# A block of attention and expert lookup on one core: TensorE's signal for a finished pair of expert sums moves from the pair's last product to a drain behind it

## What is computed

```python
def expert_chunk(args):
    xc, ic, gc = args
    u = jnp.take(u_tab, ic, axis=0)
    a = jnp.einsum('chkd,cd->chk', u, xc)
    wgt = gc * jax.nn.gelu(a)
    vv = jnp.take(v_tab, ic, axis=0)
    return jnp.einsum('chk,chkd->cd', wgt, vv)
```

## Time and profile before

| | |
|---|---|
| median of three runs | 1384.9 us |
| span of the profiled execution | 1366.9 us |
| what lies around the span (difference) | 18.0 us |
| TensorE busy | 1199.9 us, 88% |
| VectorE busy | 861.8 us, 63% |
| GpSimd busy | 500.2 us, 37% |
| ScalarE busy | 420.2 us, 31% |
| mean granted TensorE clock | 0.969 |
| moved by DMA | 405.66 MB |

### The profile page before, as it was taken

The page is one execution under the profiler, slowest core; times in us unless marked ns, Lnnn a source line. Parts: engine busy times, 40 slices in busy tenths (PEclk is TensorE's granted clock), DMA queues, the critical chain, the costliest instruction groups (busy, mean ns, idle before and its releaser), DMA issues. The chain is left out here.

```text
span 1366.9 us, 14592 instructions
## 1 busy us (share of the span) xinstructions
PE 1199.9 (88%) x4663; PEld 665.4 (49%) x4663; DVE 861.8 (63%) x1765; ACT 420.2 (31%) x1138; POOL 500.2 (37%) x580
## 2 busy tenths in 40 slices
PE   7899888888778978876788889789999999999997
PEld 4676554433344542222345433236544545999443
DVE  2657669574663654776746557679989543676345
ACT  2213334344223343343423324432323311222000
POOL 1000356666665666766666666630000000000000
PEclk9999999999998999999999999999999999999999
DMA  9998789999998999999999999986644444454450
GB/s 358 390 349 326 286 319 339 367 357 367 364 366 300 406 403 405 407 377 364 340 371 353 400 405 409 377 306 233 224 139 148 145 150 156 157 175 145 175 184 31
DMA packets 134303, 405.66 MB, mean 297 GB/s; under 512 B 10153, under 2 KB 11585, under 8 KB 133971
## 3 DMA queue, kind: packets, MB, share of 16 engines
q0 software_dynamic: 75024, 273.19, 53.1%
q1 hardware_dynamic: 57860, 127.48, 25.8%
q10 hardware_dynamic: 1342, 4.06, 0.8%
HBM read 403.12 MB, written 1.05 MB: 296 GB/s over the span
## 5 line engine op out<-in xcount | busy, mean ns | idle before, releaser
L1143 PE MATMUL psum<-gathered,modr 128*128 128x512 f32 x1024 | 505.0, 633 | 130.3 <-DMA gathered<-in_peer_v_dram,expert_idx 49.0
L2489 DVE CUSTOM_DVE_ANT_0 gathered<-gathered,psum 128x1024 f32<-128x1024 f32 x256 | 311.5, 1217 | 202.3 <-DMA gathered<-in_peer_u_dram,expert_idx 153.3
L1143 PEld LDWEIGHTS psum<-gathered,modr 128*128 128x128 f32 x1024 | 190.7, 199 | 404.7 <-issue 284.9
L687 POOL DMA_INDIRECT gathered<-in_peer_u_dram,expert_idx x256 | 244.9, 957 | 240.5 <-DVE expert_idx L1997 144.0
L701 POOL DMA_INDIRECT gathered<-in_peer_v_dram,expert_idx x256 | 242.6, 947 | 169.9 <-remote 73.7
L780 PE MATMUL psum<-featT,weight_ring 128*128 128x128 f32 (+2 forms) x960 | 145.3, 305 | 14.4 <-issue 11.3
L780 PEld LDWEIGHTS psum<-featT,weight_ring 128*128 128x128 f32 x960 | 133.7, 196 | 43.9 <-issue 35.6
L780 PE MATMUL psum<-weight_ring,featT 128*128 128x512 f32 x336 | 147.9, 596 | 1.3 <-ACT featT L1563 0.8
L1737 ACT ACTIVATE gel<-dots 128x1 f32<-128x1 f32 x256 | 51.1, 200 | 255.1 <-issue 128.1
L1746 ACT ACTIVATE modr<-ident,wgt 128x128 f32<-128x128 f32 x256 | 102.8, 402 | 18.5 <-issue 1.1
L780 PEld LDWEIGHTS psum<-weight_ring,featT 128*128 128x128 f32 x336 | 62.6, 190 | 78.8 <-issue 76.6
(11 more groups left out here) (443 smaller groups left out, 1343.1 us busy)
## 6 DMA issues: line engine op xcount, KB each, us to landing
weight_ring<-in_w_in_dram SPq DMA_DIRECT2D x16, 2048.0 KB
weight_ring<-in_w_up_dram SPq DMA_DIRECT2D x8, 2048.0 KB
weight_ring<-in_w_down_dram SPq DMA_DIRECT2D x8, 2048.0 KB
weight_ring<-in_ada_w_dram SPq DMA_DIRECT2D x5, 2048.0 KB
work<-in_ada_w_dram SPq DMA_DIRECT2D x5, 2048.0 KB, 16.3
weight_ring<-in_peer_wq_dram SPq DMA_DIRECT2D x3, 2048.0 KB
gathered<-in_ada_w_dram SPq DMA_DIRECT2D x2, 2048.0 KB, 14.5
gathered<-in_peer_u_dram,expert_idx POOLq DMA_INDIRECT x256
```

Source lines behind the costliest of these rows:

```text
L687: pool.indirect_dma_start(u_rows[:, slot, :], None, T["peer_u"], bass.IndirectOffsetOnAxis(ap=expert_idx[:, r % 2, k:k + 1], axis=0),).the ...
L1143: mm = pe.matmul(psum[:, SUM_BANK + half, :], diag[:, e % 8, :], v_rows[:, slot, 512 * half:512 * (half + 1)], start=(e % EXPERTS == 0), s ...
L2489: dve.tensor_tensor_reduce(u_rows[:, slot, :], u_rows[:, slot, :], h2_rows[t], 1.0, 0.0, ALU.mult, ALU.add, dots[:, col:col + 1])
```

## The change

`sum_expert` on TensorE no longer signals `pair_summed` at the second product of an odd step. A `drain` of TensorE stands behind that product and carries the signal. There are 128 pairs, so 128 drains are added; no matmul, transfer or wait of another engine is added or taken away.

```diff
                 for half in range(2):
-                    mm = pe.matmul(psum[:, SUM_BANK + half, :], diag[:, e % 8, :],
-                                   v_rows[:, slot, 512 * half:512 * (half + 1)],
-                                   start=(e % EXPERTS == 0), stop=(e % EXPERTS == EXPERTS - 1))
+                    pe.matmul(psum[:, SUM_BANK + half, :], diag[:, e % 8, :],
+                              v_rows[:, slot, 512 * half:512 * (half + 1)],
+                              start=(e % EXPERTS == 0), stop=(e % EXPERTS == EXPERTS - 1))
                 if e % 2:
-                    mm.then_inc(flag("pair_summed"), 1)
+                    pe.drain().then_inc(flag("pair_summed"), 1)
```

## The result

The change made the kernel slower. The median of four runs is 1397.5 us (1393.1 to 1401.6), against 1383.9 us for four runs of the kernel before (1368.9 to 1387.5; the fastest is the profiled one); the ratio is 1.0143, 95% interval 1.0098 to 1.0188. Two more measurements, on two chips and each beside the kernel before, gave 1.0137 [1.0104, 1.0169] and 1.0093 [1.0069, 1.0117]. The forecast was 1354 us, faster; the time lies inside the range of 1328 to 1400, at its far end. It is there by the room that the range left for a drain that is held a little, not by the sum.

A forecast was written before the change was run, and what follows sets the result against it. The prediction took the expert loop to be paced by arriving rows: span 1366.9 - 31.5 (late waits removed) + 0.6 (drains) = 1336.0 us, plus 18.0 around it, 1354 us against a median of 1384.9; range 1328 to 1400.

The forecast's parts named there:

- What bounds the kernel now: Expert loop, 167.6 to about 914 us: paced by row arrival, 391 to 397 GB/s in three stretches, 366 in the fourth.
- The size of a removed wait: 1.75 us of transfers behind it: Each late v-gather wait at L701 was to cost 1.75 us of lost transfers, 310 against 397 GB/s over 8 us.
- The holes of the earlier trace: Transfer rate in the 8 us from the end of six late waits: 254 to 367 GB/s, 310 on average.
- the 29: GpSimd's waits ahead of L701 put down to "remote", 73.7 us, read as late pair_summed signals that the change would remove.
- my 31.5: Gain in us from removing late v-gather waits: 18 counted at 1.75 us each; bounds nothing to 56 us.
- the likeliest case: Prompt drain in the expert loop, removing the late waits: 1354 us, spanning 1329 to 1372, chance 0.42.
- The drain's signal comes when the sums are done: Assumption behind the gain: the drain after each pair signals promptly, so the 29 late waits, 73.7 us, go.
- the held drain: Rival: drains stand as long as the late signals did, 29 x 3.4 = 99 us slower, 1484 us; chance 0.22.
- the row at 326.33: The 58th v gather, started over 8 us after its products were done; read as contradicting the skill's signal rule.
- 0.6 to 5 us: Rival: signal as late as before, only the drains' cost left; 1385 to 1390, say 1387 us; chance 0.24.
- The short cost of a drain: 0.21 to 0.35 us: TensorE's lost overlap per pair, 27 to 45 us in all, hidden in 139 us idle; 0.6 us charged.
- The 18.0 us around the span: Time outside the profiled span, taken to stay: span 1336.0 us gives 1354 against a median of 1384.9.

The follow-up runs named there:

- half_u_before: Kernel before with u gathers fetching half rows (512 numbers), half the dot product left out, same number of gathers: 1362.2 us, 0.9944.
- drain_quarter: Kernel before, signal kept at the product, with a silent drain at every eighth step only, 32 in all: 1380.1 us, 1.0086.
- drain_silent: Kernel before, signal kept at the pair's last product, with a drain without signal behind it: 1380.3 us, 1.0069.
- pad_pair: Kernel before with two added one-column matmuls of zeros ahead of the products of each odd step, no drain: 1382.3 us, 1.0040.
- drain_each_step: Changed kernel with a silent drain behind every even step too, 256 drains in all: 1443.8 us, 1.0541 against the kernel before.
- pool_long: Kernel before with a GpSimd reduction of 0.87 us behind every eighth v gather: 1376.9 us, 1.0041.
- pause_before: Kernel before with a GpSimd drain and a one-column memset behind every v gather, so hardly two gathers are in flight: 2493.4 us, 1.8162.
- drain_tail: Kernel before with 49 silent TensorE drains behind feed-forward products (L1473), outside the expert loop: 1390.7 us, 1.0152.

## Why the prediction was wrong

**"What bounds the kernel now": the loop paced by how fast rows arrive.** Wrong. Half rows of u freed the DMA engines and brought 0.56%. GpSimd's 256 steps of 2.48 us make 635 us, and with its waits they fill the loop. Loop and waits, in us:

| kernel | waits | loop | loop less waits |
|---|---|---|---|
| before | 126.0 | 746.5 | 620.5 |
| half_u_before | 122.9 | 749.1 | 626.2 |
| drain_quarter | 131.9 | 756.8 | 624.9 |
| drain_silent | 137.2 | 754.4 | 617.2 |
| pad_pair | 143.9 | 761.4 | 617.5 |
| after | 152.2 | 769.3 | 617.1 |
| drain_each_step | 202.4 | 813.1 | 610.7 |

The last column moves by 16 us, and in eleven more traces (all but those of pool_long and pause_before, where GpSimd has work added) it is 609 to 628 us. That is bookkeeping more than a law: GpSimd does nothing else in the loop, so what it doesn't wait it issues. It says that no time in the loop lies outside GpSimd's issuing and its waits, not what causes a wait, nor that a wait taken away isn't followed by another. pool_long bears the bookkeeping out: 22.3 us of waits at L701 less and 27.9 us of reductions more made its loop 7 us longer. I had the 635 us in hand, called them the bound that comes next, and left out that 635 and the 126 us of waits already make 761, slightly more than the loop.

**The size of a removed wait: 1.75 us of transfers behind it.** This step follows from the first and falls with it. The holes of the earlier trace rows were there, but bytes were not what ran short. By the bookkeeping above a signal that had really come early was worth up to 73.7 us, if no other wait had taken the place of the 29; no run took them away at full speed, so neither that figure nor my 31.5 is shown. The 1372 that I gave as the near end of the likeliest case follows from none of its bounds: with the lower bound of the gain, nothing, it would have been 1385.

**"The drain's signal comes when the sums are done", and that is early.** This is the step that turned the sign. What was late was TensorE's completion, not its message: 35 drains were held for 103 us, and 36 for 101 us with no signal on them. The sum took 31.5 us off for the early signal and put 0.6 us on for the drains; the signal did not come early, and the drains cost 13 to 20 us. My argument against the held drain was that products went on starting after 317.3, and it proves nothing, since a start doesn't need an earlier product's completion and a drain does. The observation that I weighed too lightly was the right one: two signals for two readers came free within 0.05 us. A shared moment of release points to the work or to a whole queue, not to one message.

The Trainium skill's page "Perfetto Trace Analysis", section "Tensor Engine Instruction (MATMUL, LD_WEIGHTS)", has the profile's end of a product as estimated, with PSUM's acknowledgement and the signal behind it. The traces agree as far as they reach: behind the modelled end at 633.43 the drain stood for 8.75 us more; that it is the acknowledgement that was late no run shows. I had read the row at 326.33 as speaking against that page, and it doesn't: the page says nothing of how far the real end can lie behind the estimated one. Its order, with the product's signal never later than the drain's, is what drain_silent has. The price that I had put to it, 0.6 to 5 us, was too low by the holds.

**The price of the held drain: 29 x 3.4 = 99 us, decided once drains last over 1.1 us.** The mechanism was right, with the waits at L1147 and a TensorE that stands; the size was 13 to 20 us, by the three ratios. I charged every stop with a whole pair still to do and gave it no cover, having named 139 us of idle time two paragraphs earlier. The stops took the place of 45.6 us that TensorE had stood for v rows and of 12.2 us for diagonals. The waits at L701 grew by 29.3 us with 35 held drains, so one cost about 0.8 us, not 3.4. The bound of 1.1 us a pair was a mean, and as a mean it was roughly the place: 256 drains take 111 + 256 x 0.37 = 206 us where there are 139 us of cover, and 67 us are left over; the span grew by 66.8 us. That they meet so closely is in part luck, since in that trace TensorE still stood 25.7 us for diagonals, and the medians lie 75 us apart. With 128 the sum is 103 + 47 = 150 us, about the cover itself; that the loss is what doesn't fall into the right gaps is argued, not shown.

**The short cost of a drain: 0.21 to 0.35 us, nearly all hidden.** Measured 0.36 to 0.38 us without cover, just above the upper end. What stands between a drain's end and the next product is 0.21 us ahead of a step's products (82 of the 128) and 0.06 us ahead of most others (41 of the 49 in drain_tail). "A gather that is 0.3 us later while the DMA queue is full costs nothing" is not shown either way: pad_pair's 0.4 us cost about 5 us, with an interval that reaches down to nothing.

**The 18.0 us around the span.** It was the difference between the median and a profiled execution that had taken 1368.9 us itself. Span and time of one execution lie 1.7 to 2.0 us apart in every kernel here. The forecast of the time as 1354 didn't suffer, since it was set against the median; but a sum made against a span of 1366.9 was made against the quickest of four.

**What held.** The waits at L701 are named after the drain's line, nothing outside the loop moved (1.7 of 24.5 us), and the observations that were to tell the cases apart did so: rows of microseconds for the drains, "issue" before L1143, and rates down where the earlier trace rows has 366, 391 and 397 GB/s:

```profile
250.00:350.00 100.00, 80.87 (x240) 38.91 (x239) 59.14 (x136) 37.58 (x116) 64.18 (x68) 0.93 0.96 353
422.00:500.00 78.00, 64.28 (x255) 36.32 (x255) 39.67 (x102) 22.35 (x83) 44.95 (x48) 0.96 0.97 362
...
800.00:900.00 100.00, 86.08 (x215) 37.82 (x214) 62.48 (x147) 36.10 (x115) 62.91 (x68) 0.95 1.00 384
```

## What to carry to other kernels

When a signal looks late, first ask whether the message or the work is late: two readers freed at one moment, or a silent drain behind the work, tell it for the price of one run. A drain can't report earlier than the completion that it waits for, and it stops its engine meanwhile; a wait on the instruction itself leaves the engine running. And before pricing a wait by the transfers behind it, test with a kernel that moves fewer bytes whether they pace the loop at all, and set the issuing engine's own time and its waits against the loop's length.

## What the runs showed of the hardware

- While GpSimd has many indirect gathers in flight, TensorE's completions can come microseconds behind the ends that the profile gives: 35 of 128 drains were held for 103 us, the longest for 8.75 us. In the same kernel the other 93 end some 21 ns behind the last product. With hardly two gathers in flight (pause_before) all 128 signals of the pairs came within 15 ns. With seven v slots 53 of 93 recorded ones came over 0.5 us late, with a limit of five 33 of 93, with eight slots 58 of 98.
- In the kernel before VectorE's and ScalarE's signals were not late meanwhile: all but one of 270 recorded ones came within 20 ns.
- TensorE goes on starting products meanwhile if nothing drains it; a silent drain is held as one with a signal is (36 for 101 us, 35 for 103), and it ends within 0.05 us of the late signal in 35 of 36.
- A short TensorE drain costs 0.36 to 0.38 us where nothing covers it (drain_tail, 49 drains); the next product mostly starts 0.06 us behind its end there, and 0.21 us behind it ahead of the products at L1143.
- A drain of GpSimd behind an indirect gather waits for the transfers: in pause_before GpSimd goes on 0.15 to 0.48 us behind the v row's landing, 4.5 us a step, where issuing one takes 0.94 us.
